# Rounding a block of weights whole, and making its low part whole, in place of two halves each

## The reference, cut to what matters

```python
mod = (silu(c) @ w_mod[l] + b_mod[l])                       # shifts, scales and gates
px = (rmsnorm(x, norm1_g[l]) * (1.0 + sc1) + sh1) @ w_in[l] + b_in[l]
...                                                         # the layer's mixer makes y_x from px and pc
x = x + g1 * (y_x @ w_out[l])
x = x + g2 * swiglu(rmsnorm(x, norm2_g[l]) * (1.0 + sc2) + sh2, w_gu[l], w_down[l])

def swiglu(h, w_gu, w_down):
    gate, up = jnp.split(h @ w_gu, 2, axis=-1)
    return (jax.nn.silu(gate) * up) @ w_down
```

## Time and profile before

| what | value |
| --- | --- |
| time, median of 3 runs | 2379.28 us (2376.21 to 2380.88) |
| time of the profiled execution | 2374.06 us |
| its span, first to last instruction | 2372.6 us |
| granted TensorE clock, mean | 0.969 of 2.4 GHz |
| TensorE busy | 2217.5 us, 93% |
| VectorE busy | 1086.9 us, 46% |
| ScalarE busy | 864.2 us, 36% |
| low parts of the weights (L1027) | 420 instructions, 453.1 us |
| rounding of the weights (L1692) | 420 instructions, 385.4 us |

### The profile page before, as it was taken

One profiled execution on the slowest core, in us unless ns is written; L12 is line 12 of the kernel. 1 busy time (PEld: TensorE's weight loads), 2 busy tenths in 40 slices (PEclk: granted clock), 3 DMA queues, 4 the chain that ended last, 5 costly groups with the idle time before them and its releaser, 6 DMA issues.

```text
span 2372.6 us, 28328 instructions
## 1 busy us (share of the span) xinstructions
PE 2217.5 (93%) x11868; PEld 1685.8 (71%) x11868; DVE 1086.9 (46%) x1927; ACT 864.2 (36%) x1324; POOL 0.5 (0%) x6
## 2 busy tenths in 40 slices
PE   4999698999999898799989999899999979998999
PEld 1776476777776776699956447677777757747999
DVE  3383844323232566655554433432322355555555
ACT  2344224222222544544454233422222243354443
POOL 0000000000000000000000000000000000000000
PEclk8999899999999899899999999999999989998999
DMA  9544023454446424356544002345344322202564
GB/s 337 196 150 152 1 71 117 164 160 162 160 132 207 140 89 159 108 167 207 162 145 156 1 1 71 124 163 160 126 155 127 104 72 89 72 1 89 174 201 125
DMA packets 263071, 308.09 MB, mean 130 GB/s; under 512 B 5408, under 2 KB 250272, under 8 KB 250656
## 3 DMA queue, kind: packets, MB, share of 16 engines
q1 hardware_dynamic: 256800, 299.91, 38.4%
q10 hardware_dynamic: 6144, 6.36, 0.8%
HBM read 305.21 MB, written 1.05 MB: 129 GB/s over the span
## 4 chain that ended last, share of the span: by engine, by line
PE 87%; DVE 8%; ACT 3%; issue 1%; ACTq 1%; DMA 0%; DVEq 0%
PE bank L422 86%; DVE yT L1019 2%; DVE input_low L1019 2%; DVE scratch L1019 1%; PE bank L431 1%; ACT L1682 1%; DVE big L1019 1%; ACTq L2089 0%; DMA modulation_slots<-w_mod 0%; ACT yT L1714 0%; DVE big L1423 0%; ACT rstd L1719 0%; DVE xT L1019 0%; ACT rstd L1721 0%; DVE big L1276 0%
## 5 line engine op out<-in xcount | busy, mean ns | idle before, releaser
L422 PE MATMUL bank<-input_high,weights_high 128*128 128x512 f32 (+1 forms) x2336 | 842.6, 361 | 59.6 <-DVE input_low L1019 36.5
L422 PE MATMUL bank<-input_low,weights_high 128*128 128x512 f32 (+1 forms) x2336 | 814.4, 349 | 0.0
L422 PE MATMUL bank<-input_high,weights_low 128*128 128x512 f32 (+1 forms) x2336 | 813.4, 348 | 0.0
L1027 DVE TENSOR_TENSOR weights_low<-weight_slots,weights_high 128x1024 fp32r<-128x1024 f32 (+2 forms) x420 | 453.1, 1120 | 386.4 <-ACT weights_high L1692 385.3
L422 PEld LDWEIGHTS bank<-input_high,weights_high 128*128 128x128 f32 x2336 | 447.0, 191 | 194.7 <-issue 80.3
L422 PEld LDWEIGHTS bank<-input_high,weights_low 128*128 128x128 f32 x2336 | 447.3, 191 | 61.1
L422 PEld LDWEIGHTS bank<-input_low,weights_high 128*128 128x128 f32 x2336 | 448.3, 192 | 58.8 <-issue 4.1
L1692 ACT ACTIVATE weights_high<-weight_slots 128x1024 fp32r<-128x1024 f32 (+2 forms) x420 | 385.4, 966 | 160.9 <-PE bank L422 146.5
L422 PE MATMUL bank<-hidden_high,weights_high 128*128 128x256 f32 (+1 forms) x704 | 242.8, 345 | 0.0
L422 PE MATMUL bank<-hidden_low,weights_high 128*128 128x256 f32 (+1 forms) x704 | 237.4, 337 | 0.0
L422 PE MATMUL bank<-hidden_high,weights_low 128*128 128x256 f32 (+1 forms) x704 | 237.2, 337 | 0.0
(11 more groups left out here) (229 smaller groups left out, 1580.3 us busy)
## 6 DMA issues: line engine op xcount, KB each, us to landing
modulation_slots<-w_mod SPq DMA_DIRECT2D x48, 1024.0 KB, 5.0
modulation_slots<-mod_w SPq DMA_DIRECT2D x48, 1024.0 KB, 4.9
weight_slots<-w_gu SPq DMA_DIRECT2D x44, 1024.0 KB, 5.1
weight_slots<-ffn_w_in SPq DMA_DIRECT2D x44, 1024.0 KB, 5.1
weight_slots<-w_in SPq DMA_DIRECT2D x24, 1024.0 KB, 5.3
weight_slots<-w_down SPq DMA_DIRECT2D x16, 768.0 KB, 5.0
weight_slots<-ffn_w_out SPq DMA_DIRECT2D x16, 768.0 KB, 4.9
weight_slots<-od_w_in SPq DMA_DIRECT2D x12, 1024.0 KB, 5.1
```

Of the source, the lines that this page charges most:

```text
L422: return pe.matmul(o, w, r, start=start, stop=stop, skip_group_check=shared)
L1027: tt(m.w_low[:, g % 2, c], m.ring[:, g % SLOTS, c], m.w_high[:, g % 2, c].bitcast(F32), ALU.subtract).then_inc(m.low_made.sem, 1)
```

## The change

Each block is rounded by a single ScalarE instruction and its low part is made by a single VectorE instruction. The two semaphores count blocks in place of halves. TensorE waits once, before the first step of a block's first tile, for the whole low part; the call at the middle step remains and does nothing. SyncE waits for the same moment as before, the end of the low part of block g - 4, by the new count.

```diff
-        self.high_made, self.low_made = S("weight_halves_high", (0, 2 * len(self.item))), S("weight_halves_low", (0, 2 * len(self.item)))
+        self.high_made, self.low_made = S("weight_blocks_high", (0, len(self.item))), S("weight_blocks_low", (0, len(self.item)))
...
         if g >= SLOTS:
-            sp.wait_ge(*m.low_made.at(0, 2 * (g - SLOTS) + 1))
+            sp.wait_ge(*m.low_made.at(0, g - SLOTS))
...
     def weights(g, half):
-        pe.wait_ge(*m.low_made.at(0, 2 * g + half))
+        if half == 0:
+            pe.wait_ge(*m.low_made.at(0, g))
...
         w = it.k * it.c
-        for q in range(2):
-            c = slice(q * w // 2, (q + 1) * w // 2)
-            dve.wait_ge(*m.high_made.at(0, 2 * g + q))
-            tt(m.w_low[:, g % 2, c], m.ring[:, g % SLOTS, c], m.w_high[:, g % 2, c].bitcast(F32), ALU.subtract).then_inc(m.low_made.sem, 1)
+        dve.wait_ge(*m.high_made.at(0, g))
+        tt(m.w_low[:, g % 2, 0:w], m.ring[:, g % SLOTS, 0:w], m.w_high[:, g % 2, 0:w].bitcast(F32), ALU.subtract).then_inc(m.low_made.sem, 1)
...
-        for q in range(2):
-            c = slice(q * w // 2, (q + 1) * w // 2)
-            F(m.w_high[:, g % 2, c], m.ring[:, g % SLOTS, c], ACT.Copy).then_inc(m.high_made.sem, 1)
+        F(m.w_high[:, g % 2, 0:w], m.ring[:, g % SLOTS, 0:w], ACT.Copy).then_inc(m.high_made.sem, 1)
```

## The result

The changed kernel takes 2383.74 us (median of 11 runs, 2378.61 to 2387.68), the kernel before 2375.90 us beside it (11 runs, 2374.86 to 2380.88). The ratio is 1.0031, 95% interval 1.0020 to 1.0042: 7.4 us more (4.8 to 10.0), and 7.84 by the medians. The forecast was 7.2 more, 2386.5.

A forecast was written before the change was run, and what follows sets the result against it. TensorE was taken as the bound (87% of the chain of waits); stalls at named places summed to 7.2 us, added to the 2379.28 us median for 2386.5 us. The 8-in-10 range was 2381 to 2393 us.

The forecast's parts named there:

- end of layer 1: Last residual addition stands on VectorE right behind the low part of layer 2's first block; cost 0.78 us.
- layer 3's second of the gate and up blocks: Layer 3's second gate block: low part ready for TensorE at 2191.21 against 2190.77; cost 0.44 us.
- last part: Layer 3's down part 1: a 0.47 us stall on its second block, stepped through seven blocks; cost 2.24 us.
- The price of a whole block: A 2048-wide block: 1.90 us on ScalarE, 0.03 hand-over, 2.29 on VectorE; 4.22 us whole against 3.44 in halves.
- The zero for the loads: Weights' loads issued up to 0.8 us later cost nothing, since no ScalarE row waits for a load.
- the prediction's argument on the clock: Last stretch: TensorE busy 3.50 of 3.68 us, far from the 7.64 of 11.10 before a 0.51 grant; full speed assumed.
- the ring: Layer 3's last down part: addition releases store and rounding, then conversion, next addition; 3.68 us a turn against 3.50.
- No difference: Rival: places cost the lower bound or less because rounding starts sooner; within 0.2%, up to 2384.0 us; chance 0.15.
- Faster by full queues: Rival: where VectorE's queue is full (layers 0 and 1), each block ends 0.07 us sooner; at most 2345 us; chance 0.05.
- Slower by more: Rival: gate and up blocks lack their 0.19 us margin (2390 us) or the last stretch's clock falls (2399); chance 0.15.
- the cover: Gate and up blocks of layers 1 and 3: low part ready 0.33 us early, 0.19 after TensorE's start; no stall.
- the clock would fall in the last stretch: Part of a rival (chance 0.15, mostly its other part): half the last seven blocks' 24.5 us at 1.2 GHz; 2399 us.

The follow-up runs named there:

- only the tight blocks whole: Against the kernel before: the 19 blocks with least margin before TensorE's first matmul made whole, the other 191 in halves; 2385.95 us, repeated 2383.67 us.
- The two kernels of the split: Against the kernel before: 191 blocks whole and the 19 with least margin in halves, 2376.47 us; the reverse, 2385.95 us, repeated 2383.67 us.
- the kernel with less cover: Changed kernel with 512 low-part elements made once more, ahead of the whole one, in 44 gate and up blocks of layers 1 and 3; 2399.15 us.

## Why the prediction was right

The forecast put 0.77 on slower, with 7.2 us from named places. Against it, from the two traces, block by block: how much later the first matmul of the block starts, counted from the block before it. Where the next block too starts a little later, both steps are given. At the second of the gate and up blocks the clock of before hides the step, so the wait stands there; the end of layer 1 is counted at the addition.

| place | forecast | trace of after |
| --- | --- | --- |
| layer 0's eighth block | 0 | 0.07, given back at the next |
| layer 1's fourth projection block | 0.86 | 0.87 + 0.15 |
| its seventh | 1.06 | 1.07 (wait 4.43 to 5.50) |
| layer 1's second of the gate and up blocks | not named | wait of 0.19, + 0.11 |
| second down block of part 0, layers 1 and 3 | 0.26 + 0.26 | 0.28 + 0.27 (each 0.17 or 0.16, + 0.11) |
| first gate block after it, layers 1 and 3 | 0.42 + 0.42 | 0.53 + 0.53 (each 0.45 + 0.08) |
| second down block of part 1, layer 1 | 0.47 | 0.39 + 0.11 |
| end of layer 1 | 0.78 | 0.78 |
| layer 3's second of the gate and up blocks | 0.44 | 0 here, 0.36 in the first profile with only the tight blocks whole |
| last part, seven blocks | 2.24 | 2.44 |
| sum | 7.2 | 7.7 |

So the mechanism was right, place by place: all places that it names but layer 3's second of the gate and up blocks were met within 0.2 us. What was missed goes both ways, 0.44 too much in layer 3 and some 0.9 too little elsewhere; that the two partly cancel is luck. The term that the sum lacks is the second step, 0.08 to 0.15 us behind a wait: the first matmul behind one takes 0.36 to 0.39 us where it takes 0.28 without, which is most of it.

**The price of a whole block** was exact to 0.01 us, because it was built from two sizes of the same instruction in the trace, and the hand-over of 0.03 us held too (812.86 + 1.91 to 814.80). The Trainium skill's rule (VectorE: DVE Perf Modes, The TRN2 errata: a large tile pays the fixed cost once) speaks for the change, and the busy rows bear it out: 34.5 us. The two kernels of the split show that 191 blocks together return nothing of it that can be measured. The zero for the loads held as well: in neither trace does ScalarE wait for a load of weights.

**The end of layer 1**: block 107 starts 0.19 us later in after, the addition behind the low part of block 108 goes from 1193.51 to 1194.48, 0.97 later: 0.78 of it arises there.

```profile
1192.27 2.29 DVE L1026 TENSOR_TENSOR weights_low<-weight_slots,weights_high 128x2048 fp32r<-128x2048 f32 x1 [2.14 <-ACT weights_high L1689]
...
1194.48 0.48 DVE L1020 SCALAR_TENSOR_TENSOR xT<-bank,modulation,xT 128x256 f32<-128x256 f32 x1
```

**The second of the gate and up blocks**, in layer 1 and in layer 3, are the two places where the clock decided. In layer 1 the forecast saw no stall, because in the profile of before TensorE ran at a grant of 0.51 between 1005.8 and 1009.2 and so came late; in after it ran at full speed there, came earlier, and waited 0.19 us. In layer 3 it was the other way: TensorE, at a grant of 0.51 between 2183 and 2190 us of the trace of after, came later than the low part. A margin that is read from one profile holds at that profile's clock. The same two stretches as in the earlier trace rows, in the changed kernel:

```profile
994.14:1005.24 11.10, 7.67 (x36) 5.75 (x36) 6.22 (x15) 8.35 (x19) 0.00 (x0) 1.00 0.21 73
1005.24:1008.64 3.40, 3.06 (x24) 2.66 (x23) 1.90 (x4) 3.31 (x3) 0.00 (x0) 1.00 0.00 0
```

TensorE was busy 7.67 of 11.10 us here and 7.64 of 11.10 before, and behind it the grant was 1.00 here and 0.51 there. So the prediction's argument on the clock, which compared 7.64 of 11.10 with 3.50 of 3.68, rested on a sign that doesn't decide by itself; its conclusion for the last part was right.

**The last part** was mis-sized by 0.2 us. The sum's 2.24 us came from stepping the ring and TensorE together, 0.32 us to a block and so turns of 3.82 on average; the additions "3.68 us apart" that the prediction gives as a sign are the ring's own length, and that sign was missed. The measured turns are 3.98, 3.70, 3.94, 3.75, 3.93 and 3.75: on every second turn the addition waits 0.18 us for TensorE, which was itself started late by a low part. The ring and TensorE hand the lateness to each other, and the mean is 3.84, longer than the ring alone, which took 3.70 to 3.75 in the turns where it binds. With rounding whole alone, where only the ring binds, 3.75 was worked out and 3.74 measured.

**What the clock gives and takes.** The steps sum to 7.7 us, the profiles differ by 4.55, and the medians by 7.84. Block 60 shows how. Stretches from its first matmul to that of block 61, in the kernel before and then in the changed kernel: stretch, its us, busy us by engine, granted clock, DMA share, GB/s.

```profile
846.39:860.31 13.92, 13.92 (x49) 11.07 (x49) 13.15 (x36) 0.78 (x1) 0.00 (x0) 0.79 0.31 94
```

```profile
845.34:858.01 12.67, 12.67 (x49) 10.15 (x50) 11.90 (x34) 0.78 (x1) 0.00 (x0) 0.88 0.34 102
```

The same work took 1.25 us less behind the longer stall, since the grant was 0.88 and not 0.79: as much as the stall had grown. It is no rule. Behind a wait of 5.50 us this block took 12.67, 12.72, 12.92, 13.02 and 13.06 us in five profiles, behind 5.57 us 13.33; behind 4.43 us it took 13.92, 13.87 and, with rounding whole alone, 12.81. From block 64 to block 72 most profiles are later than that of before (the changed kernel 1.24 us, four kernels 2.3 to 3.8) and three are earlier (0.6 to 0.8). Steps of 1.3 to 1.7 us of either sign stand at three or four more places; the changed kernel's profile had more of the lucky ones, which is most of the 3 us by which it and the sum differ. That they nearly cancel over many runs is suggested by the medians, which differ by about the sum. What decides in a single run how long the grant stays low behind a wait, no run here tells.

**The rivals.** No difference: the interval, 4.8 to 10.0 us, begins where that rival ended. (Its upper edge in absolute time, 2384.0, lies above the measured 2383.74, but it stood on the higher time of before.) Faster by full queues: no row for it; at block 60, the place where VectorE's queue binds, the last element did come 0.07 us sooner, but TensorE used to start with the first half. Slower by more: the cover held in all of those blocks but the one that waits 0.19 us, and the kernel with less cover shows that it was this near. That the clock would fall in the last stretch (the rule on an engine that idles shortly between groups of matmuls, in the Trainium skill, TensorE: Matmul & The Clock Gate, A second HAM failure mode: psum-queue depth-cycling) did not come about: with waits of 0.16 to 0.22 us before four of the seven blocks the grant stayed at 1.00.

```profile
2347.70:2374.40 26.70, 25.98 (x210) 24.97 (x210) 12.28 (x14) 7.66 (x6) 0.00 (x0) 1.00 0.38 109
```

## What to carry to other kernels

Cutting a producer's block in two buys overlap between the engines that work on it one after the other, and its price is a little more busy time on each (here 0.07 and 0.09 us to a block); which counts more is decided only at the blocks where the consumer is waiting, so list those with their margins before merging instructions, and price them with the full latency (rounding, hand-over, subtraction, start), not with busy time. Here 34.5 us of busy time were worth nothing that could be measured, and 19 of 210 blocks cost 7 to 8 us. Before a stall is chased, look at what the waiting engine does next: if its next wait is for the end of a chain on the same producer, taking the first wait away only moves it, and the low clock with it.

## What the runs showed of the hardware that I had not expected

- The low clock behind one and the same stall is not the same from run to run: behind 4.43 us of waiting block 60 took 13.92, 13.87 or 12.81 us, a spread as large as the loss of 1.07 us that the edit makes there. Nor does the busy share ahead decide it alone: 7.64 and 7.67 of 11.10 us busy were followed by a grant of 0.51 in one profile and of 1.00 in another. And a stall that is moved to another place can cost more than where it was: 6.28 us of waiting before the transposes made the next 13.22 us of work last 15.68, at a grant of 0.83.
- A ring and the engine that it feeds can together turn slower than either alone: a ring of 3.68 us by forecast (3.70 to 3.75 measured) and a TensorE of 3.50 us a block gave turns of 3.84.
- Single runs of one kernel differ by some 5 us (the fastest run of the changed kernel was 5.1 us below its median, at a mean grant of 0.970 for 0.967; the two profiles of the kernel with only the tight blocks whole took 2385.95 and 2381.95 us), so that a sum of steps in the trace says more about a change of 0.3% than the difference of two profiled times.
